# A decoder trunk in one TensorE stream: the last half of a weight unit's products moved in front of the transposes of the deltanet's output

## The chip, the cores and the metric

The kernel runs on one core of one Trainium2 chip. The metric is the device time of one launch in microseconds. The kernel before took 2078.51, 2078.56 and 2080.9 us in three runs, median 2078.56 us.

## The reference

Two layers of a decoder trunk, sequence length 256, width 1024, float32. Each layer normalises the residual stream, multiplies it with one wide matrix (the columns of all three token mixers and of three gates), runs the mixers, projects and gates each result, adds their sum after an output projection, and then runs a SwiGLU: dense in the first layer, top 2 of 8 experts in the second.

```python
for layer in range(DEPTH):
    h = rms_norm(x, norm_mix[layer]);  proj = h @ w_in[layer]
    (a_qkv, a_beta, a_alpha, a_gate, b_q, b_f, b_i, b_gate, c_qkv, br_gate) = split(proj)
    o_a = gated_deltanet(a_qkv, a_beta, a_alpha, a_gate, ...)   # 4 heads of 128
    o_b = hgrn2(b_q, b_f, b_i, b_gate, ...)                     # 4 heads of 128
    o_c = dilated_attention(c_qkv, ...)
    gates = sigmoid(br_gate)
    mix = gates[0] * (o_a @ w_br_a) + gates[1] * (o_b @ w_br_b) + gates[2] * (o_c @ w_br_c)
    x = x + mix @ w_out[layer]
    h = rms_norm(x, norm_ffn[layer]);  x = x + (swiglu or experts)(h)
```

The deltanet ends with `rms_norm(o, norm_g) * silu(gate)`; HGRN2 uses `f` (forget gate), `k = 1 - f`, `g = log f` summed along the sequence, and exponentials of differences of those sums. The order of the work changes here, and no value does.

## The kernel before, in words

The weights stream in as units of 1 MB (128 x 2048 float32) through six slots, `raw`. Each unit is split into two fp32r parts: ScalarE copies it to `hi` (L1165, three slots), VectorE subtracts that from `raw` and writes `lo` over it (L1652). A product with a weight is three matmuls (L481, L482, L483: hi by hi, and the two cross terms). When TensorE has used a unit up it raises `unit_used` (`unit_over`), and with that SyncE loads the unit six further on and ScalarE may make the `hi` three further on.

The order of each engine's work is written out by hand, one in-order program per engine, tied by semaphores. TensorE's program interleaves the small matmuls and transposes of the mixers (L565 and others) with products of units that later stages need, so that it has work while VectorE and ScalarE do the steps between. `group_nat` multiplies the normalised input (256 rows, two tiles of 128) with half of a 512-column group, that is one unit: 24 matmuls of 128 x 512. `group_part(pair, half, t)` does one row tile of that alone, 12 matmuls, and ends the unit with the second tile.

The end of `deltanet` (L662 to L748) issues four `group_part` calls for the first gate group: (0,0,0), (0,0,1), (0,1,0) and (0,1,1). These go to PSUM banks 0 and 1; nothing reads them until ScalarE's `gate(0)` in `hgrn` (L1413). In between stand the last small matmuls. Meanwhile VectorE and ScalarE finish the output: sum, square (L1393), reduce (L1961), two small ScalarE operations (L1395, L1397), and two VectorE products, `t_n` by the norm and `t_n` by `a_gate`, the second of which raises `o_made`. `turn_output` waits for it and issues eight transposes (L756) into banks 6 and 7, raising `o_T` after the fourth and after the eighth.

Who waits for both counts of `o_T`: ScalarE's copy to `oa_hi` (L1402), and VectorE at the head of its `hgrn`. There VectorE makes `b_k` (L1974) from `b_f` (this also raises `b_qk`), clamps `b_f` (L1976), makes `oa_lo` (L2132), splits a unit, and runs the four scans `b_gc` (L1982) when ScalarE has taken the logarithm (L1409). ScalarE's program between is: `oa_hi`, one `hi`, a table load, the logarithm, one `hi`, a table load, `gate(0)`, and the first exponentials. Then VectorE goes through eight levels, n = 0 to 7. In each it makes `b_qe` and `b_ke`, the next difference `b_e`, a masked copy out of PSUM (L1995), and one `lo`.

TensorE's `hgrn` (L761) waits at step n for `b_qk` number n, issues the small matmuls of that level (8 x 2 of 128 x 128), and then one unit of gate products, at n = 0 two. Step 0 uses `b_k` and `b_q`; step n + 1 uses the `b_ke` and `b_qe` that VectorE makes in its level n. `dilated` follows, then the projections.

Of the kernel before, what the change touches and what calls it, by code (L numbers as in the profile page):

```python
# [153 lines left out]
def build(ctx, nc, dram):  # L154
# [289 lines left out]
    def unit_view(t, k):  # L444

        return t[:, :].rearrange("p (k n) -> p k n", k=k)
# [26 lines left out]
    def _(pe):  # L473
# [5 lines left out]
        def products(out, a_hi, a_lo, b_hi, b_lo, first, last):  # L479

            pe.matmul(out, a_hi, b_hi, start=first, stop=False, skip_group_check=True)  # L481
            pe.matmul(out, a_hi, b_lo, start=False, stop=False, skip_group_check=True)  # L482
            return pe.matmul(out, a_lo, b_hi, start=False, stop=last, skip_group_check=True)  # L483

        def unit_ready(k=0):

            pe.wait_ge(hi_made.sem, prog.unit(1 + k))
            pe.wait_ge(lo_made.sem, prog.unit(1 + k))
            return hi[(prog.u + k) % SPLIT], lo[(prog.u + k) % RAW]

        def unit_over(ins):
            ins.then_inc(unit_used.sem, 1)
            prog.u += 1
# [52 lines left out]
        def group_part(pair, half, t):  # L546

            w_hi, w_lo = unit_ready()
            for k in range(4):
                a = half * 4 + k  # L550
                ins = products(PS[:, 2 * pair + t, :],
                               actT_hi[:, a, t * P:(t + 1) * P], actT_lo[:, a, t * P:(t + 1) * P],
                               unit_view(w_hi, 4)[:, k, :], unit_view(w_lo, 4)[:, k, :],
                               first=half == 0 and k == 0, last=half == 1 and k == 3)
            if t == TT - 1:
                unit_over(ins)
# [10 lines left out]
        def hs(h):  # L567
            return slice(h * P, (h + 1) * P)
# [50 lines left out]
        def mixer(L):  # L619
# [34 lines left out]
            pe.wait_ge(gate_made.sem, gate_made.at(L, 0))  # L654
            group_T(1)
            deltanet(L)
            hgrn(L)
            dilated(L)
# [3 lines left out]
        def deltanet(L):  # L662
# [81 lines left out]
            heads(lambda h: mm(PS[:, 3, hs(h)], attn[:, 1, h, :], t_m[:, 0, h, :])).then_inc(a_o.sem, 1)  # L744
            group_part(0, 0, 1)
            group_part(0, 1, 0)
            turn_output(L, 0, t_n)
            group_part(0, 1, 1)  # L748

        def turn_output(L, br, src):  # L750

            pe.wait_ge(o_made.sem, o_made.at(L, br))
            for h in range(H):
                for t in range(TT):
                    a = src[:, t, h, :] if len(src.shape) == 4 else src[:, t, hs(h)]
                    ins = pe.transpose(PS[:, (6, 2)[br] + h // 2, ((h % 2) * TT + t) * P:((h % 2) * TT + t + 1) * P],  # L756
                                       a, ident)
                if h % 2:
                    ins.then_inc(o_T.sem, 1)
# [1786 lines left out]
```

## Time and profile before

| | |
|---|---|
| time, median of three | 2078.56 us |
| the profiled execution: time | 2078.5 us |
| its span, first to last instruction | 2076.7 us |
| TensorE matmul busy | 2023.9 us (97%) |
| TensorE weight loads busy | 1727.8 us (83%) |
| VectorE busy | 1583.8 us (76%) |
| ScalarE busy | 1252.3 us (60%) |
| mean granted TensorE clock | 0.988 |

The profiled execution's time is 1.8 us more than its span. All times in the rows are from the start of the span. Matmuls overlap: the next one starts about 0.23 us after the one before, and each shows 0.39 us. The idle time in square brackets is counted from the end that the profile gives for the instruction before.

### The profile page before, as it was taken

Reading aid. Unit: us, or ns where it says so; the run is one execution under the profiler, and the core shown is the slowest. Engines: PE = TensorE matmul, PEld = TensorE weight load, DVE = VectorE, ACT = ScalarE, POOL = GpSimd, SP = SyncE. Lnnn points to the kernel's source line nnn. Section 1 sums busy time; section 2 is a strip of 40 time slices with the busy share of each in tenths; the row PEclk is TensorE's granted clock in tenths of the full one; section 3 lists DMA queues with packets and bytes.
Section 4 is the critical chain, followed back from the end, with each engine's and each line's share of the span. In section 5 each row is a group of like instructions: output and inputs, shape, how many; then the busy total and the mean of one; then the engine's idle time right before and its main releaser. Section 6 shows DMA issues by size and latency. Waiting matters only on the chain.

```text
span 2076.7 us, 28711 instructions
## 1 busy us (share of the span) xinstructions
PE 2023.9 (97%) x10743; PEld 1727.8 (83%) x10743; DVE 1583.8 (76%) x1219; ACT 1252.3 (60%) x1068; POOL 13.9 (1%) x21
## 2 busy tenths in 40 slices
PE   9999999999999999999979999999999999999997
PEld 8887888789998987888768888888888888888885
DVE  5778865755445778855767898888989888898986
ACT  5655455443345655454446777777777777777774
POOL 0000000000000000000000000000000000000000
PEclk9999999999999999999989999999999999999998
DMA  8523455255554523455238999999999999999994
GB/s 276 162 82 102 143 181 183 82 182 184 182 183 158 168 80 109 145 177 177 93 141 317 380 354 382 367 361 377 359 379 355 381 367 360 376 359 377 358 373 182
DMA packets 240494, 516.60 MB, mean 249 GB/s; under 512 B 11520, under 2 KB 34296, under 8 KB 240414
## 3 DMA queue, kind: packets, MB, share of 16 engines
q1 hardware_dynamic: 238018, 507.39, 69.1%
q0 software_dynamic: 2144, 7.88, 1.0%
q8 instruction: 55, 0.90, 0.2%
q10 hardware_dynamic: 252, 0.22, 0.0%
q14 instruction: 25, 0.20, 0.0%
HBM read 513.34 MB, written 2.12 MB: 248 GB/s over the span
## 4 chain that ended last, share of the span: by engine, by line
PE 91%; DVE 4%; ACT 2%; issue 2%; DVEq 0%; ACTq 0%
PE PS L481 27%; PE PS L483 26%; PE PS L482 26%; PE PS L565 7%; PE PS L1054 1%; ACT hi L1165 1%; PE PS L1031 1%; DVE lo L1652 1%; PE PS L806 1%; PE PS L720 0%; PE PS L1001 0%; PE PS L837 0%; DVE t_n L1675 0%; PE PS L1019 0%; DVE b_gc L1982 0%
## 5 line engine op out<-in xcount | busy, mean ns | idle before, releaser
L1652 DVE TENSOR_TENSOR lo<-raw,hi 128x2048 fp32r<-128x2048 f32 x481 | 1095.8, 2290 | 299.7 <-ACT hi L1165 297.5
L1165 ACT ACTIVATE hi<-raw 128x2048 fp32r<-128x2048 f32 x481 | 919.6, 1915 | 320.0 <-PE PS L483 313.8
L481 PE MATMUL PS<-hi,e_hi 128*128 128x512 f32 x896 | 356.2, 398 | 1.4 <-DVE e_lo L1675 1.4
L483 PE MATMUL PS<-hi,e_lo 128*128 128x512 f32 x896 | 350.4, 391 | 0.0
L482 PE MATMUL PS<-lo,e_hi 128*128 128x512 f32 x896 | 350.0, 391 | 0.0
L481 PE MATMUL PS<-hi,actT_hi 128*128 128x512 f32 x640 | 253.8, 397 | 3.7 <-DVE lo L1652 3.1
L483 PE MATMUL PS<-hi,actT_lo 128*128 128x512 f32 x640 | 249.7, 390 | 0.0
L482 PE MATMUL PS<-lo,actT_hi 128*128 128x512 f32 x640 | 249.2, 389 | 0.0
L481 PE MATMUL PS<-hi,fT_hi 128*128 128x512 f32 x536 | 208.8, 390 | 1.8 <-DVE fT_lo L1675 1.8
L483 PE MATMUL PS<-hi,fT_lo 128*128 128x512 f32 x536 | 208.7, 389 | 0.0
L482 PE MATMUL PS<-lo,fT_hi 128*128 128x512 f32 x536 | 208.7, 389 | 0.0
L483 PEld LDWEIGHTS PS<-hi,e_lo 128*128 128x128 f32 x896 | 168.8, 188 | 36.3
L481 PEld LDWEIGHTS PS<-hi,e_hi 128*128 128x128 f32 x896 | 169.0, 189 | 34.8 <-DVE e_lo L1675 1.6
L482 PEld LDWEIGHTS PS<-lo,e_hi 128*128 128x128 f32 x896 | 169.1, 189 | 33.5
L481 PE MATMUL PS<-actT_hi,hi 128*128 128x256 f32 x672 | 192.3, 286 | 0.5 <-DVE actT_lo L1675 0.5
L482 PE MATMUL PS<-actT_lo,hi 128*128 128x256 f32 x672 | 191.0, 284 | 0.0
L483 PE MATMUL PS<-actT_hi,lo 128*128 128x256 f32 x672 | 191.0, 284 | 0.0
L481 PEld LDWEIGHTS PS<-hi,actT_hi 128*128 128x128 f32 x640 | 120.3, 188 | 28.4 <-ACT hi L1165 3.9
L483 PEld LDWEIGHTS PS<-hi,actT_lo 128*128 128x128 f32 x640 | 120.2, 188 | 25.5
L482 PEld LDWEIGHTS PS<-lo,actT_hi 128*128 128x128 f32 x640 | 120.4, 188 | 23.9 <-issue 0.2
L481 PEld LDWEIGHTS PS<-actT_hi,hi 128*128 128x128 f32 x672 | 129.9, 193 | 1.9 <-issue 1.5
L482 PEld LDWEIGHTS PS<-actT_lo,hi 128*128 128x128 f32 x672 | 130.0, 193 | 0.6 <-issue 0.2
(324 smaller groups left out, 2147.1 us busy)
## 6 DMA issues: line engine op xcount, KB each, us to landing
raw<-in_moe_w SPq DMA_DIRECT2D x336, 1024.0 KB, 5.5
raw<-in_w_in SPq DMA_DIRECT2D x92, 1024.0 KB, 5.1
raw<-in_ffn_w SPq DMA_DIRECT2D x33, 1024.0 KB, 5.3
raw<-in_w_br SPq DMA_DIRECT2D x12, 1024.0 KB, 5.0
raw<-in_w_out SPq DMA_DIRECT2D x8, 1024.0 KB, 5.0
hankel<-hankel_dram POOLq DMA_DIRECT2D x1, 1536.0 KB, 12.8
x<-in_x SPq DMA_DIRECT2D x2, 512.0 KB, 5.1
f_gain<-in_norm_ffn POOLq DMA_DIRECT2D x2, 512.0 KB, 3.7
```

The costliest lines, as they stand in the source:

```text
L481: pe.matmul(out, a_hi, b_hi, start=first, stop=False, skip_group_check=True)
L482: pe.matmul(out, a_hi, b_lo, start=False, stop=False, skip_group_check=True)
L483: return pe.matmul(out, a_lo, b_hi, start=False, stop=last, skip_group_check=True)
L565: return pe.matmul(out, a, b, start=first, stop=last)
L806: ins = pe.transpose(PS[:, 4 + h // 2, ((h % 2) * TT + t) * P:((h % 2) * TT + t + 1) * P], c_n[:, t, hs(h)], ident)
L1031: ins = pe.matmul(PS[:, 4 + 2 * t + half, :], pickT[:, t, :], src[:, half * 512:(half + 1) * 512], start=part == 0, stop=part == 1)
L1054: ins = pe.transpose(PS[:, 2, j * P:(j + 1) * P], f_g[0][:, j * P:(j + 1) * P], ident)
L1165: act.activation(hi[prog.u % SPLIT][:, :], raw[slot][:, :], COPY).then_inc(hi_made.sem, 1)
L1652: dve.tensor_tensor(lo[prog.u % RAW][:, :], raw[prog.u % RAW][:, :], hi[s][:, :].bitcast(F32), ALU.subtract).then_inc(lo_made.sem, 1)
```

## The change

In the last lines of TensorE's `deltanet`, the last `group_part` call (second half of the unit's rows, second row tile, 12 matmuls and the release of the unit) goes before `turn_output` (the wait for `o_made` and eight transposes) and no longer after it. This happens once in each of the two layers. No instruction is added or removed, and no other engine's program changes.

```diff
             heads(lambda h: mm(PS[:, 3, hs(h)], attn[:, 1, h, :], t_m[:, 0, h, :])).then_inc(a_o.sem, 1)
             group_part(0, 0, 1)
             group_part(0, 1, 0)
+            group_part(0, 1, 1)
             turn_output(L, 0, t_n)
-            group_part(0, 1, 1)
```

## Rows read from the trace of the kernel before

**Rows 1.** The page, busy time by engine: us (share of the span) and instructions.
```profile
PE 2023.9 (97%) x10743; PEld 1727.8 (83%) x10743; DVE 1583.8 (76%) x1219; ACT 1252.3 (60%) x1068; POOL 13.9 (1%) x21
```

**Rows 2.** Windows: stretch, length, busy of each engine, TensorE's clock, DMA share, GB/s.
```profile
200.00:240.00 40.00, 39.30 (x219) 33.27 (x219) 39.25 (x28) 18.16 (x19) 0.00 (x0) 1.00 0.43 135
...
1400.00:1600.00 200.00, 200.00 (x917) 165.74 (x915) 178.97 (x106) 148.51 (x101) 0.94 (x1) 1.00 1.00 367
```

**Rows 3.** TensorE's timeline, first layer: start, duration, what, [idle before, releaser].
```profile
174.85 0.39 PE L483 MATMUL PS<-hi,actT_lo 128*128 128x512 f32 x1
176.41 1.09 PE L756 MATMUL PS<-consts,t_n 128*128 128x128 f32 x8 [1.17 <-DVE t_n L1675]
177.26 0.48 PE L481 MATMUL PS<-hi,actT_hi 128*128 128x512 f32 x1
...
180.09 1.95 PE L565 MATMUL PS<-b_q,b_k 128*128 128x128 f32 x16
...
192.78 1.95 PE L565 MATMUL PS<-b_qe,b_ke 128*128 128x128 f32 x16
...
199.79 0.39 PE L483 MATMUL PS<-hi,actT_lo 128*128 128x512 f32 x1
200.88 2.05 PE L565 MATMUL PS<-b_qe,b_ke 128*128 128x128 f32 x16 [0.70 <-DVE b_ke L1675]
...
208.26 2.04 PE L565 MATMUL PS<-b_qe,b_ke 128*128 128x128 f32 x16
```

**Rows 4.** TensorE's timeline: small matmuls right behind weight products.
```profile
166.41 0.39 PE L482 MATMUL PS<-lo,actT_hi 128*128 128x512 f32 x1
166.64 0.39 PE L483 MATMUL PS<-hi,actT_lo 128*128 128x512 f32 x1
166.87 1.05 PE L565 MATMUL PS<-t_w,t_y 128*128 128x128 f32 x8
```

**Rows 5.** VectorE's timeline, first layer.
```profile
175.13 1.23 DVE L1675 TENSOR_TENSOR t_n<-t_n,a_gate 128x1024 f32<-128x1024 f32 x1
177.61 0.69 DVE L1974 TENSOR_SCALAR b_k<-b_f 128x1024 f32<-128x1024 f32 x1 [1.26 <-PE PS L756]
...
182.87 2.87 DVE L1982 TENSOR_TENSOR_SCAN b_gc<-tiny,b_f 128x256 f32<-128x256 f32 x4
...
187.03 2.29 DVE L1652 TENSOR_TENSOR lo<-raw,hi 128x2048 fp32r<-128x2048 f32 x1
...
190.49 1.23 DVE L1675 TENSOR_TENSOR b_ke<-b_k,b_e 128x1024 f32<-128x1024 f32 x1
...
199.60 1.22 DVE L1675 TENSOR_TENSOR b_ke<-b_k,b_e 128x1024 f32<-128x1024 f32 x1
...
206.97 1.23 DVE L1675 TENSOR_TENSOR b_ke<-b_k,b_e 128x1024 f32<-128x1024 f32 x1
```

**Rows 6.** ScalarE's timeline, first layer.
```profile
177.54 1.12 ACT L1402 ACTIVATE oa_hi<-PS,small 128x1024 fp32r<-128x1024 f32 x1 [3.70 <-PE PS L756]
178.55 1.91 ACT L1165 ACTIVATE hi<-raw 128x2048 fp32r<-128x2048 f32 x1
...
181.77 1.06 ACT L1409 ACTIVATE b_f<-b_f 128x1024 f32<-128x1024 f32 x1
```

**Rows 7.** TensorE's timeline, second layer, the same places.
```profile
794.19 0.39 PE L483 MATMUL PS<-hi,actT_lo 128*128 128x512 f32 x1
795.81 1.09 PE L756 MATMUL PS<-consts,t_n 128*128 128x128 f32 x8 [1.23 <-DVE t_n L1675]
...
820.27 2.05 PE L565 MATMUL PS<-b_qe,b_ke 128*128 128x128 f32 x16 [0.70 <-DVE b_ke L1675]
```

**Rows 8.** SyncE's timeline, 175 to 190 us: issue of weight loads.
```profile
180.42 7.61 SPq L2405 DMA_DIRECT2D raw<-in_w_in  x2
```

**Rows 9.** TensorE's timeline behind longer waits elsewhere: the same product at both clocks.
```profile
447.07 1.97 PE L498 MATMUL PS<-consts,fn 128*128 128x128 f32 x8 [2.50 <-DVE fn L1694]
...
450.31 0.41 PE L482 MATMUL PS<-actT_lo,hi 128*128 128x256 f32 x1
...
645.11 0.28 PE L482 MATMUL PS<-actT_lo,hi 128*128 128x256 f32 x1
```

**Rows 10.** Windows around two of those products.
```profile
449.00:450.00 1.00, 0.72 (x4) 0.71 (x4) 1.00 (x3) 0.98 (x3) 0.00 (x0) 0.50 0.67 254
645.00:646.00 1.00, 1.00 (x11) 1.00 (x10) 1.00 (x3) 0.03 (x1) 0.00 (x0) 1.00 0.00 0
```

## The prediction

> **What bounds the kernel now.** I read the busy shares first. TensorE is busy 97% of the span [rows 1], so whatever leaves it idle anywhere should be found again at the end. Then the windows: in the experts' stretch TensorE is busy all of 200 us and VectorE 178.97, so there TensorE bounds. From 200 to 240 us, in HGRN2, VectorE is busy 39.25 of 40 us and TensorE 39.30 [rows 2]. A busy TensorE overlaps with itself, so this doesn't yet say who waits; the timelines do. The small matmuls of n = 2 stand behind an idle time of 0.70 us whose releaser is VectorE's `b_ke` [rows 3]. `b_ke` ends at 199.60 + 1.22 = 200.82 and TensorE starts at 200.88, 0.06 later. One level on, `b_ke` ends at 206.97 + 1.23 = 208.20 and TensorE starts at 208.26, again 0.06 later, with no idle time shown [rows 3, 5]. VectorE's period is 206.97 - 199.60 = 7.37 us and TensorE's is 208.26 - 200.88 = 7.38. What TensorE would need for itself is less: from n = 1 it goes 192.78 to its last product at 199.79, and with a step of 166.64 - 166.41 = 0.23 behind that one it could start again at 200.02, after 7.24 us [rows 3, 4]. So from n = 2 on HGRN2 runs at VectorE's pace, and TensorE's start of a level is VectorE's end of one plus 0.06.
>
> The transposes are where VectorE gets its start. Its `b_k` stands behind 1.26 us of idle time that ends with them, at 176.41 + 1.09 = 177.50, and starts at 177.61. ScalarE's `oa_hi` waits 3.70 us for the same and starts at 177.54 [rows 3, 5, 6]. From there neither engine is idle: ScalarE is at `hi` at 178.55 and at the logarithm at 181.77, its end at 182.83 releases the scans at 182.87, and from the end of the scans, 185.74, VectorE goes without a gap through a difference, a `lo` (187.03), `b_qe` and `b_ke` (190.49) [rows 5, 6]. So the transposes of the deltanet's output are the head of a chain with no slack of its own, to `b_ke` at 191.72.
>
> **The change, part by part.** It moves 12 products past a wait and eight transposes. In both layers.
>
> 1. *What it fills.* The last product before the wait starts at 174.85, so the next could start at 175.08. `t_n` is ready at 175.13 + 1.23 = 176.36 and the transposes start at 176.41: 1.33 us in which TensorE issues nothing (1.17 by the profile's count from the end) [rows 3, 5].
>
> 2. *What it delays.* The 12 products take 180.09 - 177.26 = 2.83 us behind the transposes, of which 0.10 is the first one's slower start after 128-wide ones (0.48 against 0.39 us). Behind products of their own kind they take 12 x 0.2275 = 2.73 us. They run from 175.08 to 177.81, and the transposes start there, without a wait, as the eight small matmuls do 0.23 us behind a product; these show 1.05 us and not 1.09 [rows 3, 4]. So they end at 178.86 and not at 177.50: **1.36 us later**. In the second layer 794.19 + 0.23 + 2.73 = 797.15 against 795.81, less 0.04: **1.30 us later** [rows 7].
>
> 3. *TensorE at n = 0.* It has issued the transposes at 178.66 (they take 177.26 - 176.41 = 0.85), which is 1.43 us earlier than the 180.09 of before. But `b_k` now starts at 178.86 + 0.11 = 178.97 and ends at 179.66, so TensorE starts at 179.72. The gap of 1.33 us before the transposes has become one of 1.06 us behind them; what is won is 180.09 - 179.72 = 0.37 us [rows 3, 5].
>
> 4. *TensorE at n = 1.* From n = 0 to n = 1 it took 12.69 us. With 0.10 for matmuls that start behind a wait (2.05 against 1.95 us) it arrives at 192.51. `b_ke` ends at 191.72 + 1.36 = 193.08, so TensorE starts at 193.14. The slack there was 192.78 - 191.72 - 0.06 = 1.00 us; a shift of 1.36 of the one and an arrival 0.27 earlier of the other use it up. TensorE waits 0.63 us and is 0.36 behind the old trace [rows 3, 5].
>
> 5. *TensorE at n = 2.* It arrives at 193.14 + 7.24 + 0.10 = 200.48. VectorE ends `b_ke` at 202.18. TensorE starts at 202.24, **1.36 us later** than before. From here on both have the old period, so the delay stays through n = 8, the output of HGRN2 and everything that hangs on it [rows 3, 5].
>
> 6. *The released unit.* `unit_used` comes about 2.4 us earlier. SyncE issues the next loads at about 178 and not 180.42 [rows 8]; the DMA share here is 0.43 [rows 2], so loads are neither late before nor helped now. ScalarE's next `hi` that needs the release comes after the logarithm, at 182.8: not held by it either way.
>
> What lies beside other work: nothing of the delay, since the next place where TensorE could take it up would be one where it, and not VectorE, is late, and up to n = 2 there is none. After it, all engines are shifted together. Bounds of a layer's cost: from below -1.43 us (all of step 3's earlier arrival counts and nobody is late), from above 2.73 us, the whole moved block, if `b_k` and the chain should shift by it; the row at n = 2, with 0.70 us of wait before the change, puts it at 1.36, which I take.
>
> Sum: 1.36 + 1.30 = 2.66 us against the profiled execution's 2078.5 us, which is the median of the runs shown within 0.1 us: **2081.2 us**, 0.13% more. From no change this kernel's timing can tell about 0.2%, that is 4.2 us; three runs spread over 2.4.
>
> By the Trainium skill ("Perfetto Trace Analysis", Identifying the Most-Contended Engine and Optimization Strategy) one takes the engine of the highest occupancy and makes its gaps go. By that rule, with TensorE at 97%, the change is worth its gap; that is rival A below.
>
> **The rivals.**
>
> *A, faster: the gap is what counts.* If TensorE bounds HGRN2 and VectorE has slack to give, TensorE keeps the 1.43 us of step 3 in each layer: -2.9 us, **2075.7 us**. For it speaks the 97%, and that step n = 1 shows no idle time [rows 1, 3]. Against it, the wait for `b_ke` at n = 2 that is there already, in both layers [rows 3, 7]. A half form is a delay absorbed within VectorE's chain: then step 3's 0.37 us per layer stay, 2077.8 us.
>
> *B, slower: the clock.* Behind a wait of 2.50 us the clock is at 0.50 (1.2 GHz) and eight transposes take 1.97 us; a 256-wide product takes 0.41 us there and 0.28 us at full clock (2.4 GHz) [rows 9, 10]. The change has three short waits, 1.1, 0.6 and 1.7 us, within 23 us, where one of 1.2 and one of 0.7 were. If the clock falls behind one of them, or a later stage that is shifted by 1.4 or 2.7 us meets its fall at a worse moment, a stretch like that from 447.07 to 450.31 runs at half speed, half of its 3.24 us or 1.6 us lost each time. It decides from two such stretches on: 2081.2 + 3 = **2084.2 us**, past the 0.2%. Against it: the clock is 1.00 in the window with the 0.70 us wait [rows 2].
>
> By the Trainium skill ("TensorE: Matmul & The Clock Gate", What's actually happening) the monitor's window runs free of the kernel's start, so such shifts would change the result from run to run; no run here shows that yet.
>
> *C: no net effect.* The delay lies beside something that holds TensorE later anyway, a load for one. Time **2078.5 us**. For it: nothing that I found, DMA is at 0.43 [rows 2].
>
> **How the numbers follow.** My forecast 0.72, with its own range 2079.7 to 2082.7 (the low end if the transposes or the first levels are 0.7 us per layer quicker than I have it; the high end if one clock stretch is added). A 0.07, B 0.14, C 0.07. The range for 8 in 10 is 2078.4 to 2083.8, which takes in C and most of B. Faster by over 0.2% (below 2074.4) needs more than A gives: 0.02. Slower by over 0.2% (above 2082.7): B and the top of my own range, 0.16. The rest, 0.82, is within.
>
> **What would show it.** In the changed kernel's first layer: no idle time before the transposes, which start near 177.8 us; `b_k` at 179.0 behind a wait for them; small matmuls at n = 0 behind an idle time of about 1 us, released by `b_k`, where none was; at n = 1 behind about 0.5 us, by `b_ke`; at n = 2 near 202.2 behind about 1.6 us in place of 0.70. In the second layer n = 2 starts near 820.27 + 1.36 + 1.30 = 822.9. Loads issued near 178. I am wrong if n = 2 starts before 201.5, if the delay of the first layer is gone at the start of the second's deltanet, or if the granted clock falls inside HGRN2.

## The result, and the profile after

The changed kernel took 2083.85 us (median of ten runs, 2080.81 to 2085.37) against 2078.53 us (ten runs, 2077.45 to 2084.64). The ratio is 1.0020, with a 95% interval of 1.0011 to 1.0029. The change costs 2.3 to 6.0 us. The forecast was +2.7 us and 2081.2 us. The median lies 0.05 us past 2083.8, where the range for 8 in 10 ended; by the ratio, 2078.56 x 1.0020 = 2082.7 us, it lies within it, at the upper edge of the range of my own forecast (2082.7). The profiled execution took 2082.56 us, with a span of 2080.8.

In this trace the stretch shown starts 0.87 us earlier than in that of before (`t_n` by `a_gate` at 174.26 and not 175.13), so positions are best read from a common event. The first view is TensorE's timeline after (start, duration, what, idle before and its releaser), in the first layer; it answers to [rows 3].

```profile
176.94 1.03 PE L756 MATMUL PS<-consts,t_n 128*128 128x128 f32 x8
...
178.83 2.05 PE L565 MATMUL PS<-b_q,b_k 128*128 128x128 f32 x16 [0.86 <-DVE b_k L1974]
...
192.23 2.05 PE L565 MATMUL PS<-b_qe,b_ke 128*128 128x128 f32 x16 [0.42 <-DVE b_ke L1675]
...
201.34 2.05 PE L565 MATMUL PS<-b_qe,b_ke 128*128 128x128 f32 x16 [1.58 <-DVE b_ke L1675]
...
208.72 2.05 PE L565 MATMUL PS<-b_qe,b_ke 128*128 128x128 f32 x16
```

VectorE's timeline after, for [rows 5]:

```profile
174.26 1.22 DVE L1675 TENSOR_TENSOR t_n<-t_n,a_gate 128x1024 f32<-128x1024 f32 x1
178.09 0.69 DVE L1974 TENSOR_SCALAR b_k<-b_f 128x1024 f32<-128x1024 f32 x1 [2.60 <-PE PS L756]
...
183.33 2.87 DVE L1982 TENSOR_TENSOR_SCAN b_gc<-tiny,b_f 128x256 f32<-128x256 f32 x4
...
190.95 1.23 DVE L1675 TENSOR_TENSOR b_ke<-b_k,b_e 128x1024 f32<-128x1024 f32 x1
...
200.06 1.22 DVE L1675 TENSOR_TENSOR b_ke<-b_k,b_e 128x1024 f32<-128x1024 f32 x1
```

ScalarE's and SyncE's timelines after, for [rows 6, 8]:

```profile
178.01 1.11 ACT L1402 ACTIVATE oa_hi<-PS,small 128x1024 fp32r<-128x1024 f32 x1 [5.04 <-PE PS L756]
```
```profile
177.27 9.64 SPq L2405 DMA_DIRECT2D raw<-in_w_in  x2
```

And the window that answers to the first of [rows 2]:

```profile
200.00:240.00 40.00, 38.66 (x216) 32.85 (x217) 39.21 (x29) 17.75 (x18) 0.00 (x0) 1.00 0.43 133
```

The idle time before the transposes is gone, and three waits of TensorE stand in its place: 0.86 us at n = 0, 0.42 at n = 1, and 1.58 where 0.70 was. VectorE's wait for the transposes has gone from 1.26 to 2.60 us, ScalarE's from 3.70 to 5.04: both by 1.34. From there the chain has the durations of before, and from 200 to 240 us VectorE is as full as it was while TensorE's busy time fell from 39.30 to 38.66 us. Counted from the start of the last `t_n` product, every step of the first layer can be held against the forecast:

| from the start of `t_n` by `a_gate`, us | before | forecast | after |
|---|---|---|---|
| transposes start | 1.28 | 2.68 | 2.68 |
| `b_k` starts | 2.48 | 3.84 | 3.83 |
| n = 0 | 4.96 | 4.59 | 4.57 |
| n = 1 | 17.65 | 18.01 | 17.97 |
| n = 2 | 25.75 | 27.11 | 27.08 |

Of the signs of being wrong, one came up as it was written: n = 2 starts at 201.34 us, before 201.5. It does so because the whole trace lies 0.87 us earlier there; from the common event it is 1.33 us later than before, so the sign was badly put and the delay is there.

For the experiments I call *the stage* the stretch of TensorE from the `attn` matmuls of the second chunk (168.61 us before) to the small matmuls on `b_attn` and `b_i` behind n = 8 (251.63): 83.02 us in the first layer before, 83.10 in the second. After, it is 84.32 and 84.37, **1.30 and 1.27 us more**, 2.57 together.

### The profile page after: what moved, and what is told of

Read it like the earlier page. It is cut to its first block, busy times and chain, and to the rows that moved or that the text cites. A ratio compares the mean times of both kernels' runs of the same rounds, so it can differ in the third digit from the quotient of the medians.

```text
span 2080.8 us, 28711 instructions
## 1 busy us (share of the span) xinstructions
PE 2025.8 (97%) x10743; PEld 1728.6 (83%) x10743; DVE 1583.7 (76%) x1219; ACT 1252.8 (60%) x1068; POOL 13.9 (1%) x21
## 4 chain that ended last, share of the span: by engine, by line
PE 92%; DVE 4%; ACT 2%; issue 2%; DVEq 0%; ACTq 0%
PE PS L481 27%; PE PS L483 27%; PE PS L482 27%; PE PS L565 7%; PE PS L1054 1%; ACT hi L1165 1%; PE PS L1031 1%; DVE lo L1652 1%; PE PS L806 1%; PE PS L720 0%; PE PS L1001 0%; PE PS L837 0%; PE PS L1019 0%; DVE b_gc L1982 0%; PE PS L675 0%
```

## The experiments

Each was timed against the kernel before on the same chip; 0.001 in the ratio is 2.1 us. The last column is the sum of the two layers' stages less the 166.12 us of before. In the expectations, stage E is this stage; stage D, used first, begins with the first product behind those `attn` matmuls, 0.91 us later, and differs from it by that alone.

| kernel | stage, us | ratio (95% interval) | stage sum against before |
|---|---|---|---|
| after | 84.32, 84.37 | 1.0020 (1.0011 to 1.0029) | +2.57 |
| after, again | 84.37, 84.35 | 1.0011 (1.0001 to 1.0021) | +2.60 |
| before, again | 83.03, 83.06 | 0.9995 (0.9984 to 1.0006) | -0.03 |
| first layer only | 84.35, 83.12 | 1.0009 (1.0000 to 1.0019) | +1.35 |
| block split 6 and 6 | 82.99, 83.06 | 1.0002 (0.9992 to 1.0011) | -0.07 |
| `b_k` in its own place, new order | 84.35, 84.37 | 1.0018 (1.0009 to 1.0027) | +2.60 |
| cut chain, new order | 81.03, 81.03 | 0.9984 (0.9976 to 0.9993) | -4.06 |
| cut chain, old order | 80.85, 81.23 | 0.9983 (0.9973 to 0.9993) | -4.04 |
| cut chain and table, new order | 80.32, 80.72 | 0.9978 (0.9969 to 0.9987) | -5.08 |
| cut more, new order | 79.79, 79.78 | 0.9970 (0.9959 to 0.9981) | -6.55 |
| cut more, old order | 80.85, 81.78 | 0.9990 (0.9981 to 0.9999) | -3.49 |

**1. The move in one layer.**

```diff
             group_part(0, 1, 0)
-            turn_output(L, 0, t_n)
-            group_part(0, 1, 1)
+            if L == 0:
+                group_part(0, 1, 1)
+            turn_output(L, 0, t_n)
+            if L:
+                group_part(0, 1, 1)
```

> The move in the first layer only; the second keeps the old order. Stage D is the stretch of TensorE from the first product behind the last attn matmuls to the small matmuls on b_attn and b_i; before it took 82.11 us in the first layer. Theory (the head of VectorE's chain moves, about 1.35 us a layer): stage D 83.4 us in the first layer and 82.1 in the second, time half way between before and after, about +1.3 us. Rival (the shift meets the clock's falls and that is the larger part): stage D the same as the theory has it, but the time anywhere between 0 and +5 us with low-clock stretches to match. Rival (the cost lies in the second layer, behind other loads): stage D 82.1 in the first layer.

The layer with the move has the longer stage (84.35) and the other has that of before (83.12). So each layer pays for its own move, and the second layer is not where the cost arises. The time, a median of 2082.17 us and 1.0009 of before, is between the two kernels; by itself it can't tell +1.3 from 0 (the interval begins at 1.0000).

**2. A block as long as the gap.**

```diff
             group_part(0, 1, 0)
+            group_part(0, 1, 1, (0, 1))     # the products k = 0, 1: six
             turn_output(L, 0, t_n)
-            group_part(0, 1, 1)
+            group_part(0, 1, 1, (2, 3))     # the other six, and the release
```

> Of the moved block of 12 products only 6 go in front of the transposes, 6 stay behind. 6 products last 1.37 us and the gap is 1.33, so the gap is filled and the transposes are not late. Theory (from n = 2 TensorE keeps VectorE's pace, and that hangs on the transposes): transposes 0.04 us later than before, n = 0 about 1.3 us earlier, n = 1 about 1.0 earlier, n = 2 and stage D as before within 0.1 us, time as before within 1 us. Rival A of the prediction (the gap counts): stage D 1.3 us shorter in each layer, time -2.7 us.

TensorE's timeline of this kernel:

```profile
179.93 1.07 PE L757 MATMUL PS<-consts,t_n 128*128 128x128 f32 x8
```
```profile
195.26 2.05 PE L565 MATMUL PS<-b_qe,b_ke 128*128 128x128 f32 x16 [0.17 <-DVE b_ke L1676]
...
204.36 2.05 PE L565 MATMUL PS<-b_qe,b_ke 128*128 128x128 f32 x16 [1.57 <-DVE b_ke L1676]
```

There is no idle time before the transposes and they are not late, so this is the change without its cost. Nothing is won all the same: TensorE reaches n = 0 1.36 us earlier (10.12 us after the `attn` matmuls, before 11.48), waits a little at n = 1 and 1.57 us at n = 2, and the stage is 82.99 us. The filled gap is handed back to VectorE. Rival A, by which it would have been 1.3 us a layer, is refuted here.

**3. Which way the transposes hold the chain.**

The comments in this and the next cut are explanations, and some replaced lines are left out (`...`).

```diff
-    b_k = sb("b_k", [P, H, T], at=c0 + 18432)      # over t_n and t_x
+    b_k = sb("b_k", [P, H, T], at=c0 - 4096)       # over b_o
...
-            dve.wait_ge(o_T.sem, o_T.at(L, 1))
             dve.tensor_scalar(flat(b_k), flat(b_f), -0.5, 0.5, ALU.mult, ALU.add).then_inc(b_qk.sem, 1)
```

> The new order, and b_k in a place of its own, so that VectorE makes it without waiting for the transposes; the rest of the chain as before. Stage E is now the stretch from the attn matmuls of the second chunk to the small matmuls on b_attn and b_i (before 83.02 and 83.10 us in the two layers, with the new order 84.32 and 84.37). Theory (the chain goes through ScalarE: oa_hi, hi, table, logarithm, and the scans wait for that): the idle time at n = 0 goes, the one at n = 1 grows from 0.4 to some 1.3 us, n = 2 and stage E stay, 84.3 us in each layer, time as with the new order. Rival (the wait for b_k at n = 0 is what the new order costs): stage E 83.4 us, time as before the change.

TensorE's timeline of this kernel; ScalarE's logarithm; VectorE's `lo` and scans; and what VectorE waited for from 165 to 262 us (waiter, releaser, us, times, longest):

```profile
178.24 1.95 PE L565 MATMUL PS<-b_q,b_k 128*128 128x128 f32 x16
...
192.66 2.05 PE L565 MATMUL PS<-b_qe,b_ke 128*128 128x128 f32 x16 [1.59 <-DVE b_ke L1675]
```
```profile
182.67 1.06 ACT L1409 ACTIVATE b_f<-b_f 128x1024 f32<-128x1024 f32 x1
```
```profile
181.39 2.29 DVE L1652 TENSOR_TENSOR lo<-raw,hi 128x2048 fp32r<-128x2048 f32 x1 [0.44 <-ACT hi L1165]
183.76 2.87 DVE L1981 TENSOR_TENSOR_SCAN b_gc<-tiny,b_f 128x256 f32<-128x256 f32 x4
```
```profile
DVE oa_lo L2131 <- ACT oa_hi L1402: 2.3, 1, 2.3
```

The wait at n = 0 is gone, and the one at n = 1 is 1.59 us (I had expected some 1.3). From the `attn` matmuls, n = 1 comes after 24.51 us, with the new order alone after 24.49. The stage is 84.35 us, as with the new order. So `b_k` and the wait at n = 0 cost nothing; the chain goes through ScalarE, which makes `oa_hi`, a `hi`, the table and the logarithm behind the transposes. The scans stand behind two branches of it that end 0.05 us apart: the logarithm at 183.73, and at 183.68 VectorE's own `oa_lo` and `lo`, which wait for `oa_hi` and `hi`. To shorten only one of them would gain next to nothing.

**4. and 5. The chain cut, in both orders.** `b_k` as above, and besides (the old lines for clamp, table and logarithm in `hgrn`, which these replace, are not shown):

```diff
+            # VectorE, in its wait for the squares
+            dve.tensor_scalar(flat(b_f), flat(b_f), 1e-18, None, ALU.max).then_inc(b_clamp.sem, 1)
...
+            # ScalarE, in its wait for the transposes; the scans read b_ke
+            act.preload_act_table_set(LN_SET)
+            act.wait_ge(b_clamp.sem, b_clamp.at(L))
+            act.activation(flat(b_ke), flat(b_f), LN).then_inc(b_g.sem, 1)
             turn_output(L, 0)
...
             diff(0)
-            prep(1)
+            split_output(L, 0)      # these stood in front of the scans
+            prep(2)
```

> The new order, with the chain behind the transposes cut: b_k has its own place and is made without waiting for them, the clamp of b_f stands in VectorE's wait for the squares, ScalarE takes the logarithm (into b_ke's place) in its wait before the transposes, and oa_lo and one lo go behind the scans. VectorE then ends its first b_ke some 2.7 us earlier than before. Theory: with that slack the moved block is pure gain, no idle time of TensorE before the transposes, at n = 0, 1 or 2, stage D 82.11 - 2.9 = 79.2 us in each layer, time -5.8 us against before (2072.7). Rival (something else than this chain delays n = 2, for instance hi, lo or the PSUM banks): stage D stays at 82 or more, and time as before or above.

> The same cut chain with the old order of products and transposes. Theory: the gap of 1.3 us before the transposes stays, the wait at n = 2 goes, stage D 82.11 - 1.7 = 80.4 us in each layer, time -3.4 us against before (2075.1); so here the new order is worth -1.2 us a layer, where without the cut it cost +1.35: the sign of the change turns with the slack of the chain. Rival (the moved block costs by itself, by whatever it does to TensorE or the clock): this kernel is faster than the one with the new order.

Both are faster than before, which confirms the chain. But my expectation for their order fell: 81.03 and 81.03 us with the new one, 80.85 and 81.23 with the old, in sum 162.06 and 162.08. As stage D that is 80.1 us with the new order where I had expected 79.2, and 79.9 and 80.3 with the old where I had expected 80.4. The new order is no longer a loss and not yet a gain: it is 0.18 us behind in the first layer and 0.20 ahead in the second. The first layer's gap is smaller here to begin with: the reduction of the squares starts 0.11 us behind ScalarE's square (171.01 to 171.12) where before it was 0.46 (171.58 to 172.04), and the gap before the transposes is 0.83 us and not 1.17. The clamp that now stands in VectorE's wait for the squares is what differs there; why the reduction starts sooner behind it is not shown. VectorE's and ScalarE's timelines of the cut kernel with the new order:

```profile
186.59 1.23 DVE L1675 TENSOR_TENSOR b_qe<-b_q,b_e 128x1024 f32<-128x1024 f32 x1 [0.62 <-ACT b_e L1422]
```
```profile
178.23 1.12 ACT L1405 ACTIVATE oa_hi<-PS,small 128x1024 fp32r<-128x1024 f32 x1 [3.01 <-PE PS L756]
179.24 3.71 ACT L1165 ACTIVATE hi<-raw 128x2048 fp32r<-128x2048 f32 x2
182.97 1.28 ACT L1413 ACT_TABLE_LOAD   x1
184.27 1.03 ACT L1413 ACTIVATE gate<-PS 128x1024 f32<-128x1024 f32 x1
185.19 0.66 ACT L1420 ACTIVATE b_e<-b_e 128x512 f32<-128x512 f32 x1
185.89 0.67 ACT L1422 ACTIVATE b_e<-b_e 128x512 f32<-128x512 f32 x1
```

And the kernel with the old order, ScalarE, then TensorE:

```profile
176.62 1.12 ACT L1405 ACTIVATE oa_hi<-PS,small 128x1024 fp32r<-128x1024 f32 x1 [1.33 <-PE PS L756]
```
```profile
175.49 1.09 PE L756 MATMUL PS<-consts,t_n 128*128 128x128 f32 x8 [0.83 <-DVE t_n L1675]
...
191.85 1.95 PE L565 MATMUL PS<-b_qe,b_ke 128*128 128x128 f32 x16
199.09 1.95 PE L565 MATMUL PS<-b_qe,b_ke 128*128 128x128 f32 x16
```

I had cut VectorE's chain from the transposes and left ScalarE's: `oa_hi` still waits for them, and the exponentials for `b_qe` stand behind it, two `hi`, a table and a gate. With the new order they end at 186.56, VectorE waits 0.62 us (0.20 in the second layer), and from n = 2 TensorE is at VectorE's pace again. With the old order they are in time (they end at 184.95 us, `b_qe` starts at 185.96) and TensorE goes at its own, 199.09 - 191.85 = 7.24 us a level, but keeps the gap before the transposes.

**6. ScalarE's part cut too.** One line more on kernel 4:

```diff
             act.activation(flat(b_ke), flat(b_f), LN).then_inc(b_g.sem, 1)
+            act.preload_act_table_set("exp_and_others")
```

> The cut chain with the new order and only the table load moved. In the first cut kernel with the new order VectorE waited 0.62 us (first layer) and 0.20 us (second) for ScalarE's exponentials. Theory: those waits go, VectorE's pace still sets the levels, stage E 81.03 - 0.6 = 80.4 us and 81.03 - 0.2 = 80.8 us, time -4.9 us against before. Rival (the exponentials do not matter, TensorE meets something else at n = 2): stage E 81.0 in both.

80.32 and 80.72 us: what VectorE had waited, and 0.1 us more. In the first layer the levels n = 1 to 5 are 7.24 us apart, the later ones 7.38. So the new order now leads the old one of kernel 5 by 0.5 us in each layer. The table load was not moved by itself in the old order; there TensorE went at its own pace already.

**7. and 8. The fill of `b_attn` off VectorE too, in both orders.**

```diff
-                    dve.memset(flat(b_attn), 0.0).then_inc(dve_step.sem, 1)
...
+            pool.wait_ge(a_r1.sem, a_r1.at(L))
+            pool.memset(b_attn[:, :, :, :].rearrange("p a b c -> p (a b c)"), 0.0).then_inc(pad_made.sem, 1)
```

> The cut chain with the new order, and two cuts more, since there VectorE waited for ScalarE's exponentials and then kept its own pace of 7.38 us a level from n = 2: ScalarE loads the table for exponentials in its wait before the transposes, and GpSimd fills b_attn with zeros in place of VectorE. Theory: VectorE has some 1.5 us of slack at n = 2, TensorE goes at its own 7.24 us a level without any gap from the attn matmuls on, stage E 79.8 us in each layer, that is -3.2 and -3.2 against before, time -6.4 us. Rival (TensorE still meets VectorE's pace before n = 8): 80.4 to 81.0 us. Rival (GpSimd's fill slows VectorE while both use SBUF): VectorE's operations between 164 and 170 us longer than in the kernel before, and the transposes later.

> The same cuts with the old order. Theory: TensorE was already at its own pace with the first cut, so nothing is gained over that kernel: stage E 80.9 and 81.2 us, time -4 us against before; the new order is worth 1.0 and 1.3 us here, the gap before the transposes, and with it the sign of the change has turned. Rival (the new order never pays): this kernel as fast as or faster than the one with the new order.

With the new order, TensorE's timeline in the first layer and the window that answers to [rows 2]:

```profile
181.58 1.04 PE L756 MATMUL PS<-consts,t_n 128*128 128x128 f32 x8
...
195.14 1.95 PE L565 MATMUL PS<-b_qe,b_ke 128*128 128x128 f32 x16
202.38 1.83 PE L565 MATMUL PS<-b_qe,b_ke 128*128 128x128 f32 x15
```
```profile
200.00:240.00 40.00, 40.00 (x225) 34.83 (x224) 39.21 (x29) 18.80 (x20) 0.00 (x0) 1.00 0.42 133
```

(The view ends inside the last group, of which it shows 15 of 16.) No idle time is left from 200 to 240 us, the stage is 79.79 and 79.78 us as expected (79.8), and the time is 0.9970 of before, median 2071.44 us: **the fastest of the kernels here**, its mean 6.3 us below that of the runs of before beside it. With the old order the stage is 80.85 and 81.78. So the same move of 12 products costs 1.30 and 1.27 us a layer in the kernel as it was, is worth 0.0 with the first cut, and gains 1.06 and 2.00 us with the last. In the second layer 0.55 us of that, and of the 81.78 us where I had expected 81.2, go with GpSimd's fill (below): the old order shows it, the new one hides it. Without that the gain there is some 1.45 us. Both are about the gap that the old order has left in front of its transposes, 0.85 and 1.78 us by the profile's count.

**9. and 10. Both kernels once more.**

> The changed kernel itself once more. Its first ten runs stood 4.1 us above before (2.3 to 6.0), of which the chain explains 2.6 (stage E: 1.30 and 1.27). Theory (the rest is chance: the clock's low stretches fall differently in each execution): the ratio comes out nearer to 1.0013, between 0 and 5 us above, and the profile has stage E 84.3 us again in each layer with low-clock stretches at other places than in the first profile. Rival (the shift of the later stages against something regular costs 1.5 us more by itself): again 4 us or more.

> The kernel before against itself, to see what the comparison makes of no change: ratio 1.000, interval about 0.001 to each side; stage E 83.0 and 83.1 us; the start (to the attn matmuls of the second chunk, 168.6 us in the first profile) anywhere between 167.7 and 172.4 us, as in the profiles so far.

The stages repeat within 0.05 us. The times do not repeat so well: the ratio of the changed kernel is 1.0011 this time, though its median, 2083.73 us, is again 5.1 us above that of before (2078.62) and its mean 3.2, and before against before gives 0.9995 with 0.0011 to each side. So neither of my two expectations for the repeat is decided by the time. The other half of the theory came out: the repeat has low-clock stretches where the first profile had none, one from 2060 to 2063 us for example, and its time behind the second stage is 1.84 us longer (table below).

## Why the prediction was right, and where not

**What it fills, what it delays (steps 1 and 2): right.** The gap is gone, the transposes end 1.34 and 1.28 us later in the two layers (forecast 1.36 and 1.30), and the time at which they start was forecast to 0.01 us. The split block shows the first half alone: filling the gap moves nothing at n = 2.

**n = 0, n = 1, n = 2 (steps 3 to 5): right** within 0.04 us each, as the table above has it. Kernel 3 adds what I had not told apart: I named `b_k` as the wait at n = 0 and, beside `oa_hi`, as the start of VectorE's chain, and the part that counts is ScalarE's. The arithmetic came out the same since both wait for the same transposes.

**The released unit (step 6): right**, loads go out 3.0 us after `t_n` starts and not 5.3, and behind the `attn` matmuls TensorE waits in both stages for VectorE alone, never for a load, before and after.

**The sum: mechanism right, size short by what the clock does.** 2.66 us forecast, 2.57 in the stages. But the time rose by 4.2 us by the ratio and by 5.3 by the medians, and that is the part of the prediction that missed: its sum put what happens outside the two stages at nothing and left it to rival B. The two profiled spans differ by 2080.8 - 2076.7 = 4.1. The rest lies outside the stage, where both kernels do the same work: -0.87 us in front of the first, +2.27 between them and +0.13 behind the second.

| us | to the stage of layer 1 | between the stages | behind the second |
|---|---|---|---|
| before | 168.61 | 536.32 | 1205.65 |
| before, again | 168.68 | 536.39 | 1205.64 |
| after | 167.74 | 538.59 | 1205.78 |
| after, again | 167.97 | 537.29 | 1207.62 |
| first layer only | 172.40 | 536.13 | 1205.80 |
| block split | 172.11 | 534.89 | 1205.95 |
| cut more, new order | 172.37 | 538.28 | 1205.88 |

So in these seven stretches with one and the same order of work vary by up to 4.7, 3.7 and 2.0 us. The windows at the start of the second layer show how (stretch, length, busy times, granted clock third from the end); before, then after:

```profile
641.00:645.00 4.00, 3.77 (x20) 3.40 (x21) 2.82 (x5) 3.97 (x7) 0.00 (x0) 0.57 0.41 150
645.00:650.00 5.00, 5.00 (x44) 5.00 (x43) 5.00 (x4) 0.03 (x1) 0.00 (x0) 1.00 0.01 3
```
```profile
642.00:646.00 4.00, 3.54 (x19) 2.94 (x19) 2.92 (x5) 3.92 (x6) 0.00 (x0) 0.61 0.40 154
646.00:650.00 4.00, 4.00 (x22) 4.00 (x22) 4.00 (x4) 0.00 (x0) 0.00 (x0) 0.54 0.01 4
```

The first product of that stretch and the 21st, before, then after:

```profile
644.43 0.49 PE L481 MATMUL PS<-actT_hi,hi 128*128 128x256 f32 x1 [0.23 <-DVE actT_lo L1675]
...
647.02 0.28 PE L483 MATMUL PS<-actT_hi,lo 128*128 128x256 f32 x1
```
```profile
645.33 0.55 PE L481 MATMUL PS<-actT_hi,hi 128*128 128x256 f32 x1 [0.34 <-DVE actT_lo L1675]
...
649.72 0.27 PE L483 MATMUL PS<-actT_hi,lo 128*128 128x256 f32 x1
```

Behind the same wait of 2.7 us the clock fell in both to 0.50 (1.2 GHz; windows of 1 us show it from 642 to 644 us before and from 643 to 649 after), before for the transposes and hardly beyond them, after for the products behind them too: 22 matmuls in 4 us where before had 44 in 5. From the first of these products to the 21st it is 2.59 us before and 4.39 after, 1.80 more; from there to the second stage both take 140.93 us. The other 0.47 of the 2.27 us had come up by the first product. So in this pair of profiles the excess between the stages is time at the low clock, and not other work. That is rival B's second form, a shifted stage that meets the fall at a worse moment; its first form, a fall inside HGRN2, is refuted (after, clock 1.00 from 160 to 300 us and from 790 to 875). That the median, 2083.85, stands nearer to B's 2084.2 than to my 2081.2 us doesn't make B's sum right: it had the 2.66 us of the chain and two whole stretches of 1.6. The Trainium skill ("TensorE: Matmul & The Clock Gate", What's actually happening) has the monitor's window run free, so that this is chance from run to run. Part of it must be: the two profiles of the changed kernel differ in it (the slow products behind that wait last to 649.7 us in the one and to 646.9 in the other, 1.30 us of difference between the stages), and the runs of before fall into clusters, 60 of 97 below 2079.4 us, 25 between that and 2083, 12 above. But the two profiles of before have their falls at the same places to 1 us, none of the 22 runs of the changed kernel is below 2080.8, and in two sets the changed kernel's mean is 2083.4 (22 runs) and that of before 2079.5 (97 runs), 3.9 us apart and not 2.6. Whether the remaining 1.3 us is a lasting effect of the shift on where the clock falls, or chance, stays open. It isn't peculiar to the new order: each of the ten comparisons with a changed program has a mean above what its stages give, by 0.3 to 1.6 us, the old order with the cuts by 0.9 and 0.7. And before against itself differed by 1.2 us in the mean, the other way.

**The rivals.** A (2075.7 us) was given 0.07 and did not happen, though it has the right mechanism for a kernel with slack: with the last cut the new order gains about its gap, 1.06 us and, without GpSimd's part, some 1.45 where A had 1.43. C (no net effect) is refuted by the stages. The rule that led to A, the busiest engine's gaps first, held only once VectorE's and ScalarE's parts of the chain were cut.

## What to carry to other kernels

A gap on the busiest engine is worth filling only with work that ends when the awaited thing comes: what is behind the wait may be the head of another engine's chain. Look one or two waits further down for an idle time that is there already; if it is, a filled gap is handed back there and a delayed hand-over is paid in full. And try such a move again once that chain is shorter: its sign can turn, as here from a cost of 1.3 us a layer to a gain of 1.1 in the first layer. A chain is cut only when every engine on it is cut: after VectorE's part was free, ScalarE's still carried the delay.

## What the runs showed of the hardware

GpSimd's fill of `b_attn` (1.38 us) ran beside four `tensor_scalar` of VectorE on `b_f` in the second layer. VectorE in the cut kernel without the fill on GpSimd, then VectorE and GpSimd with it, both in the old order:

```profile
783.83 1.76 DVE L1947 TENSOR_SCALAR b_f<-b_f,lb 128x256 f32<-128x256 f32 x4
```
```profile
784.36 2.29 DVE L1948 TENSOR_SCALAR b_f<-b_f,lb 128x256 f32<-128x256 f32 x4
```
```profile
783.78 1.38 POOL L2374 MEMSET b_attn<- 128x1536 f32 x1 [337.72 <-DVE t_w L1676]
```

The four took 2.29 us and not 1.76, and all of that is in the first of them: 0.95 us, the others 0.41 each as without the fill (with the new order 0.95 and 0.41 too). In the first layer the fill ran beside a `tensor_tensor` from PSUM (0.68 us with and without it) and a `lo` (2.29 both), and nothing was longer. I had expected, as a rival, that VectorE would be slowed between 164 and 170 us; it was not there but in the second layer. The Trainium skill ("SBUF — State Buffer", SBUF: two separate sides) has GpSimd and some forms of VectorE instructions lock each other out of a shared port. The trace agrees in that only the instruction that met the fill was longer, and that it ended at 785.31 us, behind the fill's end at 785.16. The 0.53 us are less than the 0.80 of the fill that were left when it started; starts and ends on GpSimd are rough in a profile, so how long it was held isn't settled, and that it was this port is not shown.
